# Layers of an attention stack: compressed scores one slot later, four products with V in the slots of score groups

## The reference, cut to what matters

```
k_cmp = _compress(kc, pe_k, w1_k, w2_k)
s_c = einsum('bqghd,bngd->bghqn', qb, k_cmp) + head_bias(dist_c)
p_c = _masked_softmax(s_c, dist_c >= 0)
o_c = einsum('bghqn,bngd->bqghd', p_c, v_cmp)
...
inner = einsum('bnchd,bnehd->bnhce', qc, kc) * decay
o_inner = einsum('bnhce,bnehv->bnchv', inner, vc)
```

## Time and profile before

| | |
|---|---|
| median of 3 runs | 1145.68 us (1145.44 to 1145.97) |
| profiled execution | 1145.91 us, its span 1144.1 us |
| PE busy | 1134.6 us, 99% of the span |
| DVE / ACT / POOL busy | 823.8 / 587.5 / 140.2 us |
| granted clock of TensorE | 0.998 over the span |
| wide panels of layer 0, of layer 1 | from 346.82 to 474.77 us, from 774.70 to 903.00 us |

### The profile page before, as it was taken

The page is one execution under the profiler, slowest core; times in us unless marked ns, Lnnn a source line. Parts: engine busy times, 40 slices in busy tenths (PEclk is TensorE's granted clock), DMA queues, the critical chain, the costliest instruction groups (busy, mean ns, idle before and its releaser), DMA issues.

```text
span 1144.1 us, 15970 instructions
## 1 busy us (share of the span) xinstructions
PE 1134.6 (99%) x6208; PEld 949.7 (83%) x6208; DVE 823.8 (72%) x1253; ACT 587.5 (51%) x742; POOL 140.2 (12%) x152
## 2 busy tenths in 40 slices
PE   9999999999999999999999999999999999999997
PEld 7888777788997777888888888997777888888886
DVE  6665666567699899787777454699899786777443
ACT  7555566544525676534455333426676534555332
POOL 1321232100003234000000000003234000000000
PEclk9999999999999999999999999999999999999999
DMA  9645535367545678654555655445677654555641
GB/s 360 233 177 194 217 146 183 121 231 258 169 149 211 190 213 221 184 183 156 213 184 186 217 199 195 168 160 201 190 207 221 186 182 167 201 188 190 223 154 38
DMA packets 35180, 219.35 MB, mean 192 GB/s; under 512 B 3872, under 2 KB 5408, under 8 KB 10784
## 3 DMA queue, kind: packets, MB, share of 16 engines
q1 hardware_dynamic: 33232, 205.72, 51.1%
q0 software_dynamic: 1728, 12.58, 5.9%
q10 hardware_dynamic: 144, 0.01, 0.0%
HBM read 217.25 MB, written 1.05 MB: 191 GB/s over the span
## 4 chain that ended last, share of the span: by engine, by line
PE 78%; issue 15%; DVE 3%; DVEq 1%; ACT 1%; DMA 1%; POOL 0%; POOLq 0%; SPq 0%; ACTq 0%
PE panel L992 31%; PE panel L998 16%; PE panel L1066 5%; PE panel L958 5%; PE tile L1080 4%; PE panel L1069 3%; PE panel L1043 3%; PE panel L1042 3%; PE panel L1041 3%; DVE area L2297 2%; PE heads_out L1283 1%; PE tile L1344 1%; PE heads_out L1430 1%; DMA area<-in_first_chunks_dram 1%; DVEq L2298 1%
## 5 line engine op out<-in xcount | busy, mean ns | idle before, releaser
L650 DVE TENSOR_TENSOR ring_parts<-ring,ring_parts 128x2048 fp32r<-128x2048 f32 (+1 forms) x170 | 387.4, 2283 | 154.5 <-ACT ring_parts L606 151.0
L606 ACT ACTIVATE ring_parts<-ring 128x2048 fp32r<-128x2048 f32 (+1 forms) x182 | 344.9, 1898 | 255.3 <-PE panel L998 187.7
L992 PE MATMUL panel<-ring_parts,hT 128*128 128x512 f32 (+1 forms) x1184 | 291.6, 392 | 0.0
L992 PEld LDWEIGHTS panel<-ring_parts,hT 128*128 128x128 f32 x1184 | 212.7, 188 | 47.9 <-issue 7.2
L992 PE MATMUL panel<-ring_parts,area_parts 128*128 128x512 f32 x736 | 177.4, 389 | 0.0
L992 PEld LDWEIGHTS panel<-ring_parts,area_parts 128*128 128x128 f32 x736 | 137.9, 188 | 28.5
L998 PE MATMUL panel<-ring_parts,hT 128*128 128x512 f32 (+1 forms) x592 | 151.0, 390 | 0.0
L1066 PE MATMUL panel<-hT,ring_parts 128*128 128x512 f32 x512 | 129.9, 393 | 0.0
L998 PEld LDWEIGHTS panel<-ring_parts,hT 128*128 128x128 f32 x592 | 107.4, 188 | 23.3 <-issue 2.5
L2297 DVE SCALAR_TENSOR_TENSOR area<-area,cw 128x256 f32<-128x256 f32 x240 | 105.0, 499 | 2.8
L1066 PEld LDWEIGHTS panel<-hT,ring_parts 128*128 128x128 f32 x512 | 91.6, 189 | 16.0
(11 more groups left out here) (255 smaller groups left out, 1231.7 us busy)
## 6 DMA issues: line engine op xcount, KB each, us to landing
ring<-in_w_layers_dram SPq DMA_DIRECT2D x140, 1024.0 KB, 4.9
ring<-in_w_first_dram SPq DMA_DIRECT2D x38, 1024.0 KB, 5.0
ring_parts<-in_w_layers_dram POOLq DMA_DIRECT2D x12, 1024.0 KB, 8.7
area<-in_second_bias_dram SPq DMA_DIRECT2D x8, 320.0 KB, 3.2
ring<-in_w_layers_dram SPq DMA_DIRECT2D x4, 560.0 KB, 3.9
ring<-in_w_first_dram SPq DMA_DIRECT2D x4, 512.0 KB, 9.5
area<-in_first_bias_dram SPq DMA_DIRECT2D x4, 384.0 KB, 4.4
area<-in_later_bias_dram SPq DMA_DIRECT2D x1, 1536.0 KB, 12.1
```

The costliest lines, as they stand in the source:

```text
L606: act.activation(ring_lo[:, SLOTS + hi, 0:w], ring[:, slot, 0:w], ACT.Copy).then_inc(high_ready, 1)
L650: g.tensor_tensor(ring_lo[:, slot, 0:w], ring[:, slot, 0:w], ring_lo[:, SLOTS + hi, 0:w], ALU.subtract).then_inc(low_ready, 1)
L992: pe.matmul(ps[:, b, 0:width], t[:, 4 * i + k, b * P:(b + 1) * P], hi[:, k, :], start=(i == k == 0 and t is of[0]), stop=False)
```

## The change

Only the two plan lines change. Products with V: pair 1 from slot 15 to 18 (ahead of S3), pair 2 from 22 to 23 (ahead of S4), pair 4 from 40 to 36 (ahead of S6), pair 5 from 43 to 44 (ahead of S7). Compressed scores: cmpS from slot 19 to 20, where it is alone, cmpN from 21 to 22, PcT from 23 to 24, where it is alone. R0 stays in slot 19, behind T4 and T5, and R2 in slot 21.

```diff
-LAYER_V = (8, 15, 22, 29, 40, 43, 51, 55)
+LAYER_V = (8, 18, 23, 29, 36, 44, 51, 55)
 LAYER_SUM, LAYER_HIGH = (29, 57), (30, 61)
-LAYER_OTHER = dict(cmpHk=5, cmpFk=8, ro0=11, ro1=6, cmpHv=12, cmpFv=14, rot=17, cmp2=17, cmpS=19, cmpN=21, PcT=23, R0=19, R2=21, Or0=33, Or1=30, oR=48, cv=58, cz=62)
+LAYER_OTHER = dict(cmpHk=5, cmpFk=8, ro0=11, ro1=6, cmpHv=12, cmpFv=14, rot=17, cmp2=17, cmpS=20, cmpN=22, PcT=24, R0=19, R2=21, Or0=33, Or1=30, oR=48, cv=58, cz=62)
```

## The result

The changed kernel takes 1152.19 us (median of 4 runs, 1150.58 to 1153.18), the kernel before 1145.59 beside it: a ratio of 1.0054 [1.0042, 1.0067], slower by 6.6 us. The prediction, 1149.9 in [1147.2, 1153.0] and slower, holds. Its forecast is 2.3 us too low, and that part has causes of its own.

A forecast was written before the change was run, and what follows sets the result against it. PE, almost never waiting, was taken as the bound, with DVE just ahead. A 3.0 us wait per layer at PcT, less later savings, left 1.9 and about 2.3: plus 4.2 us, 1149.9, range 1147.2 to 1153.0.

The forecast's parts named there:

- The wait at PcT: Slot 24, each layer: PE ready at 401.7 but DVE's coefficients end at 404.7, so PE waits 3.0 us.
- 0.1 for its form: Slot 19: R0, now directly after T5 on PE, pays 0.1 us for its change of form.
- the 0.25 for semaphores: DVE's tap of slot 20: 0.25 us more, as semaphores are now read behind the drain.
- Merges of 0.25: Four slots per layer: a V directly ahead of an S saves PE 0.25 us each, between 0 and 0.27.
- The rival that merging does nothing: A V ahead of an S saves nothing: plus 5.2 us, 1150.9; chance 0.06.
- POOL's 1.2 us: Taps of slot 21: POOL's multiplication still runs inside them, so 1.2 us stays in their 4.62.
- POOL misses the taps: Rival: multiplication falls elsewhere, PcT waits only 1.8 us; plus 1.9, 1147.6; chance 0.12.
- Behind slot 25: After slot 25, PE's 2.9 us lateness stays, less 0.5 from V4 and V5; T13's wait goes in layer 1.
- Transfers have the panels as cover: Weight transfers behind the wait: the panels cover them, so they add no time.
- The clock: Rival: each 3 us wait halves PE's clock for 5.3 us, costing 2.7 each; 1155.3; chance 0.10.
- The sum: Whole kernel: plus 4.2 us, from 1.9 in layer 1 and about 2.3 in layer 0.
- the gain survives: Rival: wait at PcT below 0.5 us, PE keeps 0.5 a layer, 1144.7, not slower; chance 0.07.

The follow-up runs named there:

- cmpn_21: The changed kernel with the compressed coefficients (cmpN) back in slot 21, ahead of the decays of R2: 1148.24 us, ratio 1.0019.
- taps_22: The changed kernel with DVE's two taps of slot 21 moved to slot 22, directly behind the compressed coefficients: 1149.23 us, ratio 1.0032.
- cmps_19: The changed kernel with the compressed scores (cmpS) back in slot 19, between T5 and R0: 1147.80 us, ratio 1.0015.
- v_only: The kernel before with only the four products with V moved: 1145.47 us, ratio 0.9997.
- after_again: The changed kernel run once more, unchanged: 1152.48 us, ratio 1.0051.
- v_tap: The kernel before with the four products with V moved and two taps moved from slot 31 to slot 46: 1143.38 us, ratio 0.9977.

## Why the prediction was right, and where it was short

- *The wait at PcT, 3.0 us per layer.* Right in kind and nearly in size: 2.59 and 2.58, and slot 25 at 58.41 against 55.59 in layer 1, 2.82 behind where 2.9 was said. The end of L2439, said for 404.7, was 404.55, 57.95 from the panels' start where 57.9 was said. Errors inside cancel. R0 behind T5 was put at 0.1 for its form; it waits 0.41 idle for ACT's copy of T4's tile. cmpS stands behind it on PE, so DVE got it 0.35 later than said (46.9 against 46.6 from the panels' start) and stood 1.89 instead of 1.4. This was wrong, and not harmless, as DVE's chain hangs on cmpS. Against it, the 0.25 for semaphores were 0.07 (395.34 to 397.15, 1.81 against 1.74), and the two taps with their drain took 4.54 (398.22 to 402.76) where I said 4.7. That the sum came out within 0.1 us is luck. cmpn_21, taps_22 and cmps_19 take its main terms away: the decays with the taps, the taps, and the stand.
- *Merges of 0.25.* Right: 0.25 each in v_only, four times in each layer. The rival that merging does nothing falls.
- *POOL's 1.2 us.* Right in place: the multiplication ran inside the taps (399.69 for 1.52). Undisturbed, the two taps take 3.41 (taps_22), so it cost 1.21 before and 1.05 here; in taps_22 it adds 1.29 to what it meets. cmpn_21 shows that the decays, with one input in PSUM, go on beside it. So "POOL misses the taps" had about the right price, and was not what happened. The rule of the Trainium skill, page "SBUF — State Buffer", section "SBUF: two separate sides", names the same exclusion; the trace agrees, now for the decays too.
- *Behind slot 25.* Slot 46 is 2.38 late in layer 1, as said (2.4), and T13's wait is gone. In after_again, whose layer 1 has neither a fall of the clock nor a wait in slot 46, that layer takes 130.16 us, 1.86 more than before, where 1.9 was said. "Transfers have the panels as cover" is the sentence that failed. Before, the transfer of mg3/1 landed 1.25 and 0.76 us ahead of the first product that uses it; in layer 1 of the changed kernel that product waited for it. It cost 0.99 there and 0 to 0.23 in the other three layers profiled. The transfer hangs on a root of POOL, and this on DVE, but DVE's lateness isn't what cost: POOL issued it 1.55 us later, PE came 2.38 later, and the transfer took 10.86 us instead of 8.44. Layer 1, first the kernel before, then the changed one (SP issues the transfers of the other halves):

```profile
859.06 7.53 SPq L790 DMA_DIRECT2D ring<-in_w_layers_dram  x2
...
866.21 6.44 SPq L790 DMA_DIRECT2D ring<-in_w_layers_dram  x2
...
867.61 0.94 POOL L2658 DMA_DIRECT2D ring_parts<-in_w_layers_dram  x1
```

  Before, POOL's issue (862.62) came 3.56 us behind one of SP's, now 1.40. Over the 28 transfers of mg3/1 in the fourteen profiled executions this divides them: seventeen issued within 1.5 us of one of SP's, before or behind it, took 9.3 to 11.4 us, the other eleven 8.2 to 9.0. No run changed this distance alone, so that the two transfers hinder each other is likely and not shown.
- *The clock.* I gave it 0.10 as a rival with 2.7 us for each wait. It came in part: three falls in six places, 1.4 to 1.6 us each. With a fall in every second place and 1.5 us for each, an estimate from these six, 1.5 us belonged in the sum. The price of 2.7 was too high because a fall lasted 3.41 us and not the 5.3 of the start. The Trainium skill, page "TensorE: Matmul & The Clock Gate", section "Why this matters for your kernels", warns of idle gaps; here a gap of 2.3 to 2.6 us was enough, some of the time.
- *The sum.* +4.2 was said against +6.6. In the profiled execution the panels took 6.54 more. Of these 1.41 are the fall of the clock and 1.01 the wait for the transfer in slot 46 (0.02 and 0.99), two terms that the sum put at nothing; the remaining 4.12 are what it did hold. In after_again the panels took 5.88 more, 1.59 by the fall and 0.23 in slot 46, which leaves 4.06. For the runs without a trace this split is likely and not shown. So the mechanism and its price were right, and the median lies in the range because its upper half had room, for one fall among other things.

The rival "the gain survives" needed the 2.5 us of DVE's chain not to be there. They are, and v_only adds that even without this chain no gain that shows would have been left.

## What to carry to other kernels

When steps are moved to later slots, walk the list of the engine that works just ahead of the bound one. A producer moved one slot back makes the follower stand, and here hardly any of that time was made up (0.2 of 1.6 us in cmpn_21): it came back at the next tile or at the last consumer. A gain on the bound engine is only real if the engine just ahead can give it up too; here two taps moved behind the next hand-over turned nothing that shows into a gain of 2.6 us (ratios 0.9997 and 0.9977).

## What was not expected of the hardware

- The granted clock fell to half for 3.41 us after PE had idled little more than 2 us, in three of six equal places, twice only when PE was back at work; not after 1.35 us (two places).
- Ten extra products of 128x512 in the idle time cost nothing, and in their profile the clock didn't fall.
- POOL's multiplication holds up a DVE instruction of 128x8 elements as long as a big one: 1.54 us for two instead of 0.25; in cmps_19 one TENSOR_SCALAR of 128x16 took 1.30 instead of 0.17.
- Transfers issued by POOL for equal halves landed 8.4 us after issue before, 10.9 in the changed kernel and 11.4 in v_tap (all layer 1, mg3/1). The long ones were all issued within 1.5 us of one of SP's transfers, the short ones were not.
